# Two stacked transformer blocks on one core: work at eight seams between stages, and the order inside attention, rearranged

## The chip, the core and the metric

The kernel runs on one core of one Trainium2 chip. The core has five engines with queues of their own: TensorE (PE; its weight loads, PEld, overlap the matmuls), VectorE (DVE), ScalarE (ACT), GpSimd (POOL) and SyncE (SP), which here issues nearly all DMAs. Each engine takes its instructions in order and waits on counting semaphores. The metric is the device time of one execution in microseconds. All data are float32.

## The reference

The input is x (512 tokens of width 1024), a context of 256 tokens and conditioning vectors. Two blocks follow each other:

```
first_block:   h = modulate(rms_norm(x))
               hgrn2 branch: 4 heads, chunked gated linear scan, both directions
               deltanet branch: 4 heads, 2-D conv, gated delta rule, both directions
               x = x + g1 * (concat(gated_head_norm(o) for both branches) @ w_out)
               x = x + g2 * hierarchical_moe(modulate(rms_norm(x)))   # 16 experts, top 2
second_block:  layer 0: attention over ctx+lat (768 keys, 512 queries), then conv_ffn
               layer 1: sgu_mixer, then conv_ffn; last an rms_norm
gated_head_norm(o, gate, w) = rms_norm(o, w) * silu(gate)          # per head of 128
attention: 4 differential heads (two 64-wide maps each, p = p1 - lam * p2, then
           rms_norm over the head, *0.8) and 8 query heads of 64 on 2 KV heads;
           each layer: x = x + g1 * mixer(...);  x = x + g2 * conv_ffn(...)
sgu_mixer: z = gelu(h @ w_in); u, v = split(z); v = rms_norm(v)
           mixed = w_s (4 groups of 128x128, per chunk of 128 tokens) @ v + b_s
           return (u * mixed) @ w_out
conv_ffn:  z = h @ w_up; 3-tap conv over tokens; (silu(g) * u) @ w_down
```

## The kernel before, in words

**Stages.** The kernel is one program of thirteen stages in a fixed order: norm1, hg0, hg1, dn0, dn1, wout, moe, proj, attn, awout, ffn0, sgu, ffn1. Each engine has its own function for each stage (`pe_attn`, `act_attn`, `dve_attn`, `pool_attn`, and so on), and the order within an engine is written out by hand. After each stage every engine but SP calls `meet` (L207 to L211):

```
def meet(eng, who):
    k = meetings[who] = meetings.get(who, 0) + 1
    eng.drain().then_inc(s["stage_done"], 1)
    eng.wait_ge(s["stage_done"], 4 * k)
```

So none of the four starts a stage before all have ended the one before. SP isn't in the meetings; it runs ahead with the weight chunks (1 MB each, a ring of six slots, `Stream`), and waits for `stage_done` in two places, after moe (for attention's small tables) and after ffn0 (for sgu's).

**Tiles.** Tokens are in four tiles of 128 (NX = 4). `hT` holds the normed input transposed (8 chunks of 128 channels by 512 tokens), `xres` the residual, `ps` is PSUM with eight banks of 512 floats a partition. One product of a stage (`L694`, `L2450`, `L3029`) is eight contraction steps of 128 into one 128 x 256 block; a 128 x 512 one is in two halves of 4 steps. Each float32 matmul shows as two records in the trace.

**dn1.** The inverse of the delta rule's triangular systems is a loop of units u over levels and chunks (DVE L1588, POOL's masks L1416, PE L1173 to L1201), then come five state steps k (PE L1221 to L1247, POOL's `kx` L1458), then the outputs of four chunks (DVE L1648, semaphore `do_out`).

**The output stages** wout (j = 0), awout (j = 1) and the end of sgu (j = 2) share `pe_out`, `act_out`, `dve_out`, `pool_out`. `pe_gate_rows` (L476) makes the gate of all channels a row of every partition with 32 small matmuls into banks 0 to 3; ACT copies them out (`gate_rows_out`). For each token tile m: DVE prepares the source (`prep`), PE turns it (L1724), ACT and DVE copy the turned halves to `hT`, PE does two half products (L1734, 16 records each), DVE multiplies by the gate (L1802), POOL adds to `xres` (L1832), ACT sums the squares (L1681), DVE scales by the root (L1701), PE turns that tile again (L1674, the renorm) and ACT and DVE write it with scale and shift to `hT` (L1688, L1706), where the next stage reads it. The renorm of tile m - 1 stands behind the products of tile m, that of the last tile behind all.

**prep** of wout is: square, sum over each of eight heads, mean and epsilon, (ACT: root), times the silu gate `gz`, times the norm's weight in two halves, reciprocal, product (L1876 to L1885). That of awout does the same for the four differential heads (L2723 to L2731), that of sgu adds the bias to the mixed values and multiplies (L3085).

**proj and attention.** proj makes 36 products of 128 x 256 in six banks; the other two take heads being turned (L2466). Attention has 32 units: (group g, head h, query tile m); g = 0 are the differential heads, g = 1 the grouped ones. A unit is: scores of two maps over 768 keys into banks 0 to 3 (L2592, each map on its own 64 rows of the array), two maxima on DVE (L2663), two exps on ACT (L2643), reciprocals (L2684), for g = 0 the combination on DVE (L2687, L2689), for g = 1 a scaling of one map on DVE (L2694) and of the other on POOL (L2701), the turns of the probabilities (L2607), their copies (ACT L2652 and L2654, DVE L2681), the product with the values (L2619 or L2623) and its copy out (L2671, L2673). PE's order is scores u + 1, values u - 1, turns u.

**ffn.** Each pair of 128-wide column blocks of w_up is computed by seven products of half size (L2842) instead of eight, from sums and differences of weights (`weight_sums`, L2928 to L2932) and of token halves (`xsum`, L2935 to L2939). Products 0 and 1 take the first 256 tokens as they are; product 2 is the first that needs sums. Then come the down products, with the second half tile by tile and the renorms behind (layer 0).

**sgu.** 32 products of 128 x 256, each through Gelu (L3057), the four column groups of v first; then gate rows, the turn of the mixing weights (L3040), the four mixes (L3048, 8 records each) and `pe_out` with j = 2.

## Time and profile before

| what | value |
|---|---|
| median of 3 runs | 2980.68 us (2980.64 to 2988.81) |
| profiled execution | 2980.87 us, its span 2978.8 us |
| PE busy | 2763.9 us, 93% |
| DVE, ACT, POOL busy | 39%, 21%, 16% |
| mean granted clock of TensorE | 0.972 |
| DMA | 403.12 MB, mean 135 GB/s |

The span is from the first to the last instruction that the profiler recorded. A row of the timeline merges neighbouring instructions of one kind: start, time, engine, line, what it writes and reads, how many, and in brackets how long the engine had been idle and who released it. The granted clock is TensorE's in shares of full speed; it has two levels, 1.0 (2.4 GHz) and 0.5 (1.2 GHz), and values between are means over a stretch.

### The profile page before, as it was taken

Reading aid. Unit: us, or ns where it says so; the run is one execution under the profiler, and the core shown is the slowest. Engines: PE = TensorE matmul, PEld = TensorE weight load, DVE = VectorE, ACT = ScalarE, POOL = GpSimd, SP = SyncE. Lnnn points to the kernel's source line nnn. Section 1 sums busy time; section 2 is a strip of 40 time slices with the busy share of each in tenths; the row PEclk is TensorE's granted clock in tenths of the full one; section 3 lists DMA queues with packets and bytes.
Section 4 is the critical chain, followed back from the end, with each engine's and each line's share of the span. In section 5 each row is a group of like instructions: output and inputs, shape, how many; then the busy total and the mean of one; then the engine's idle time right before and its main releaser. Section 6 shows DMA issues by size and latency. Waiting matters only on the chain.

```text
span 2978.8 us, 35816 instructions
## 1 busy us (share of the span) xinstructions
PE 2763.9 (93%) x14509; PEld 2052.2 (69%) x14509; DVE 1168.4 (39%) x2158; ACT 613.9 (21%) x1186; POOL 465.5 (16%) x499
## 2 busy tenths in 40 slices
PE   7999988988985999999999887899999999999998
PEld 4676655776752788788778665588864685788843
DVE  2173662663353111111134575476720002677601
ACT  2102021332312111111131354121100121211100
POOL 2152502636401000000010023111101001011100
PEclk9999998999997999999999999999999999999999
DMA  9211141434632999999952100122221320322220
GB/s 371 88 43 43 67 171 46 142 128 144 213 117 101 354 331 334 320 330 335 319 176 71 43 1 1 57 90 94 85 66 48 111 84 15 120 85 85 78 78 28
DMA packets 202879, 403.12 MB, mean 135 GB/s; under 512 B 12882, under 2 KB 100482, under 8 KB 193538
## 3 DMA queue, kind: packets, MB, share of 16 engines
q1 hardware_dynamic: 195554, 375.15, 36.7%
q10 hardware_dynamic: 4896, 17.83, 1.5%
q0 software_dynamic: 2304, 8.39, 0.7%
q8 instruction: 89, 1.46, 0.2%
q14 instruction: 36, 0.29, 0.0%
HBM read 369.88 MB, written 31.46 MB: 135 GB/s over the span
## 4 chain that ended last, share of the span: by engine, by line
PE 69%; issue 21%; DVE 4%; ACT 3%; DMA 1%; POOL 1%; ACTq 0%; SPq 0%; POOLq 0%; DVEq 0%
PE ps L2842 18%; PE ps L702 7%; PE ps L1734 5%; PE ps L2856 5%; PE ps L2450 4%; PE ps L3029 4%; PE ps L2871 4%; PE ps L694 3%; PE ps L393 2%; PE ps L1173 2%; PE ps L1187 2%; PE ps L774 2%; PE ps L2592 2%; DMA ring<-in_w_mod 1%; ACT arena L2643 1%
## 5 line engine op out<-in xcount | busy, mean ns | idle before, releaser
L2021 PEld LDWEIGHTS ps<-arena,ring 128*128 128x128 f32 x2944 | 334.3, 193 | 13.5 <-issue 10.5
L2021 PE MATMUL ps<-arena,ring 128*128 128x128 f32 x2944 | 334.6, 276 | 2.6 <-DMA ring<-in_w_gate 2.6
L2842 PE MATMUL ps<-arena 128*128 128x256 f32 x1056 | 235.3, 379 | 3.2 <-DVE arena L2939 3.2
L2842 PEld LDWEIGHTS ps<-arena 128*128 128x128 f32 x1056 | 200.5, 190 | 31.2 <-DVE arena L2939 4.0
L1734 PE MATMUL ps<-ring,hT 128*128 128x512 f32 x384 | 173.7, 609 | 4.1 <-DVE arena L3085 2.6
L702 PE MATMUL ps<-hT,ring 128*128 128x512 f32 x384 | 172.1, 603 | 4.6 <-ACT ring L1312 2.1
L2842 PE MATMUL ps<-hT,ring 128*128 128x256 f32 x704 | 163.3, 386 | 3.3 <-ACTq L210 3.3
L2039 PE MATMUL ps<-ring,arena 128*128 128x512 f32 x368 | 164.0, 598 | 1.8
L2856 PE MATMUL ps<-ring,arena 128*128 128x512 f32 x352 | 151.5, 592 | 1.3 <-issue 1.3
L2842 PEld LDWEIGHTS ps<-hT,ring 128*128 128x128 f32 x704 | 136.4, 194 | 23.3 <-ACTq L210 4.1
L2871 PE MATMUL ps<-ring,arena 128*128 128x512 f32 x352 | 151.7, 592 | 0.0
L1416 POOL TENSOR_TENSOR arena<-arena,levm 128x256 f32<-128x256 f32 x168 | 128.8, 789 | 93.7 <-PE ps L1173 81.7
L1734 PEld LDWEIGHTS ps<-ring,hT 128*128 128x128 f32 x384 | 73.7, 196 | 91.7 <-issue 89.4
L2988 POOL TENSOR_TENSOR arena<-arena 128x512 f32<-128x512 f32 x44 | 56.7, 1288 | 509.8 <-DVE arena L2949 509.8
L2310 DVE TENSOR_TENSOR arena<-arena,ps 128x512 f32<-128x512 f32 x23 | 15.8, 687 | 303.9 <-PE ps L2021 303.9
L702 PEld LDWEIGHTS ps<-hT,ring 128*128 128x128 f32 x384 | 73.1, 193 | 89.8 <-issue 83.5
L2450 PE MATMUL ps<-ring,hT 128*128 128x256 f32 x576 | 125.3, 379 | 1.6 <-ACTq L210 1.6
L2039 PEld LDWEIGHTS ps<-ring,arena 128*128 128x128 f32 x368 | 68.0, 190 | 84.2 <-issue 84.2
L2856 PEld LDWEIGHTS ps<-ring,arena 128*128 128x128 f32 x352 | 66.7, 190 | 85.2 <-issue 85.2
L2871 PEld LDWEIGHTS ps<-ring,arena 128*128 128x128 f32 x352 | 66.7, 190 | 83.2 <-issue 83.2
L2450 PEld LDWEIGHTS ps<-ring,hT 128*128 128x128 f32 x576 | 109.0, 190 | 16.5 <-ACTq L210 1.9
L3029 PE MATMUL ps<-ring,hT 128*128 128x256 f32 x512 | 113.4, 385 | 1.6 <-ACTq L210 1.6
(485 smaller groups left out, 4196.6 us busy)
## 6 DMA issues: line engine op xcount, KB each, us to landing
ring<-in_ada_w SPq DMA_DIRECT2D x48, 1024.0 KB, 4.9
ring<-in_w_gate SPq DMA_DIRECT2D x46, 1024.0 KB, 7.2
ring<-in_w_up SPq DMA_DIRECT2D x46, 1024.0 KB, 6.5
ring<-in_w_down SPq DMA_DIRECT2D x46, 1024.0 KB, 5.3
ring<-in_ffn_w_up SPq DMA_DIRECT2D x44, 1024.0 KB, 5.1
ring<-in_w_mod SPq DMA_DIRECT2D x24, 1024.0 KB, 7.5
ring<-in_ffn_w_down SPq DMA_DIRECT2D x20, 1024.0 KB, 5.0
ring<-in_w_in SPq DMA_DIRECT2D x18, 1024.0 KB, 7.4
```

Of the source, the lines that this page charges most:

```text
L393: last = pe.matmul(ps[32 * b:32 * b + 32, mod_bank(g), :], sil[:, k, :], w[:, 0, b * BANK:(b + 1) * BANK], start=(k == 0), stop=(k == KD - ...
L694: last = pe.matmul(ps[:, bank, 0:CW], hsrc[:, k, m * P:(m + 1) * P], w[:, k, :], start=(k == 0), stop=(k == KD - 1))
L702: last = pe.matmul(ps[:, bank, 0:n], w[:, k, j * P:(j + 1) * P], src[:, k, :], start=(k == 0), stop=(k == KD - 1))
L1416: last = g.tensor_tensor(al[u % 2][:, 2 * d:2 * d + 2, :], AT[:, c, 2 * d:2 * d + 2, :], bc(levm[:, l, d, :], [P, 2, P], 1), ALU.mult)
L1734: last = pe.matmul(ps[:, 2 * (m % 2) + half, :], hT[:, 4 * q + k, m * P:(m + 1) * P], ws[2 * half + q][:, k, :], start=(q == 0 and k == 0) ...
L2021: last = pe.matmul(ps[:, t, f * P:(f + 1) * P], w[:, k, f * P:(f + 1) * P], xg[:, 4 * c + k, :], start=(c == 0 and k == 0 and f == 0), sto ...
L2039: last = pe.matmul(ps[:, 2 + half, :], aT[:, 2 * c + k, :], w[:, k, half * 512:(half + 1) * 512], start=(c == 0 and k == 0), stop=(c == 1 ...
L2450: last = pe.matmul(ps[:, u % PB, 0:CW], hT[:, k, m * P:(m + 1) * P], w[:, k, :], start=(k == 0), stop=(k == KD - 1))
L2842: last = pe.matmul(ps[:, u % 8, 0:HTOK], a[:, k, :], b[:, k, :], start=(k == 0), stop=(k == KD // 2 - 1))
L2856: last = pe.matmul(ps[:, m, :], fa[:, q + k, m * P:(m + 1) * P], w[:, k, :], start=(q + k == 0), stop=(q + k == NF - 1))
L2871: last = pe.matmul(ps[:, 4 + m, :], fa[:, q + k, m * P:(m + 1) * P], ws[i][:, k, :], start=(q + k == 0), stop=(q + k == NF - 1))
L3029: last = pe.matmul(ps[:, u % 8, 0:CW], hT[:, k, m * P:(m + 1) * P], w[:, k, :], start=(k == 0), stop=(k == KD - 1))
```

## The change

`meet` gets a parameter that leaves the waiting out; it is left out behind dn1, proj, attn, awout, ffn0 and sgu, and the dependences that it covered have semaphores of their own. Pieces of one stage move into the neighbour:

- dn1 and wout: DVE squares and sums the four hg heads at four units of dn1's inverse (u = 8, 14, 20, 26); POOL multiplies the gates `gz` by the norm's weights behind the state steps k = 1 to 4; `prep` is left with half the square and sum. ACT loads the table of the root early and does tile 0's root ahead of the gate rows.
- proj and attention: banks are given out anew in proj's last eight products (`proj_bank`), so that scores 0 stand before product 33 and scores 1 before product 35, and the first exps between proj's last copies.
- attention: the scores are signalled and awaited by map; from unit 17 on DVE's copy of the turned probabilities stands behind the next reciprocal and scaling.
- attention and awout: squares and weights of the differential heads go to POOL, sums to DVE, the root to ACT, all in units 17 to 31; `prep` is one product.
- awout and ffn0, sgu's output and ffn1: `pe_ffn_ahead` puts products 0 and 1 ahead of the last renorm, the first weight sums stand around the last tile's scaling, and the token differences are signalled in two parts.
- ffn0 and sgu: `pe_sgu_ahead` puts sgu's product 0 ahead of the last renorm, and products 1 to 3 wait for tiles, not for the stage.
- sgu and its output: gate rows before product 14, the weights' turn before 25, mixes 0 to 2 before 28, 29, 30, mix 3 behind the first turn.

The diff, cut to its core:

```diff
-        def meet(eng, who):
+        def meet(eng, who, wait=True):
             eng.drain().then_inc(s["stage_done"], 1)
-            eng.wait_ge(s["stage_done"], 4 * k)
+            if wait:
+                eng.wait_ge(s["stage_done"], 4 * k)
...  (pool_dn, dve_dn)
+                if p and k:
+                    for b in range(2):
+                        x = gz[:, k - 1, 512 * b:512 * b + 512].rearrange("p (h x) -> p h x", x=P)
+                        last = g.tensor_tensor(x, x, bc(hgw[:, b, :], [P, 4, P], 1), ALU.mult)
+                if p and u in WO_SUMS_AT:
+                    ch.link(v.tensor_tensor(wo_sq[:, 0:4], x, x, ALU.mult))
+                    ch.link(v.reduce_sum(hss[:, m, 0:4], wo_sq[:, 0:4], axis=X))
...  (pe_out)
             turn(0)
+            if between:
+                between()
+            if j < 2:
+                pe.wait_ge(s["gate_out"], j + 1)
...
+            if ahead:
+                ahead()
             renorm(NX - 1)
...  (dve_wout)
-                ch.link(v.tensor_tensor(wo_sq, o, o, ALU.mult))
-                ch.link(v.reduce_sum(hss[:, m, :], wo_sq, axis=X))
+                ch.link(v.tensor_tensor(wo_sq[:, 4:8], o[:, 4:8], o[:, 4:8], ALU.mult))
+                ch.link(v.reduce_sum(hss[:, m, 4:8], wo_sq[:, 4:8], axis=X))
...
-                for b in range(2):
-                    ob = o[:, 4 * b:4 * b + 4, :]
-                    ch.mark(v.tensor_tensor(ob, ob, bc(hgw[:, b, :], [P, 4, P], 1), ALU.mult))
...  (proj)
+        def proj_bank(u):
+            return u % PB if u < 28 else 4 + u % 2 if u < 32 else 6 + u % 2
+                    if u in (32, 33):
+                        pe.wait_ge(s["heads_act"], (n + 1) // 2)
+                        pe.wait_ge(s["heads_dve"], n // 2)
...
+                    if u == 33:
+                        pe.wait_ge(s["ap_out"], CTX_UNITS + 28)
+                        attn_scores(pe, 0)
+                    if u == 35:
+                        attn_scores(pe, 1)
...  (attention)
+        def attn_scores(pe, u):
+            for a, c0, c1 in ((0, 0, BANK), (1, 0, BANK), (0, BANK, TOK), (1, BANK, TOK)):
+                if u and c0 == 0:
+                    pe.wait_ge(s["exp_done"], 2 * u - 1 + a)
+                last = pe.matmul(...)
+                if c1 == TOK:
+                    last.then_inc(s["score2_ps"], 1)
-                if 1 <= u <= AU:
-                    (wait, copy of the turned probabilities of u - 1)
+                if 1 <= u <= ND or u == AU:
+                    turn_out(u - 1)
                 if u < AU:
                     (reciprocals, combination or scaling)
+                if ND < u < AU:
+                    turn_out(u - 1)
...  (pool_attn, i = u - 16)
+                if 1 <= i <= 2 * NX:
+                    m, weighed = divmod(i - 1, 2)
+                    if not weighed:
+                        g.tensor_tensor(ao_sq[m % 2], o, o, ALU.mult).then_inc(s["probs_pool"], 1)
+                    else:
+                        g.tensor_tensor(o, o, bc(subw[:, :], [P, 4, P], 1), ALU.mult).then_inc(s["probs_pool"], 1)
...  (ffn)
+        def pe_ffn_ahead(pe, W, l):
+            pe.wait_ge(s["h2_act"], renormed(2 + 2 * l, 2))
+            pe.wait_ge(s["h2_dve"], renormed(2 + 2 * l, 2))
+            pe.wait_ge(s["gated"], 8 * (1 + l) + 6)
+            for u in range(2):
+                up_product(pe, W, u, *seven_products(w, 0)[u])
...  (dve_ffn; the products wait for the first part at 2, for the second at 3)
+            ch.link(v.tensor_tensor(xsum[:, 0], tokens_part(0, 1), tokens_part(0, 0), ALU.subtract))
+            v.wait_ge(s["h2_act"], renormed(2 + 2 * l, NX))
+            v.tensor_tensor(xsum[:, 1], tokens_part(1, 1), xsum[:, 0], ALU.subtract).then_inc(s["sums_ready"], 1)
...  (pe_sgu)
+                if u == 14:
+                    pe.wait_ge(s["gelu_out"], 12)
+                    pe_gate_rows(pe, 2, False)
+                if u == 25:
+                    (turn of the mixing weights)
+                if 28 <= u < 31:
+                    mix(u - 28)
+                sgu_unit(pe, W, w, u)
+            pe_out(pe, W, 2, so, lambda: pe_ffn_ahead(pe, W, 1), lambda: mix(3))
```

## Rows read from the trace of the kernel before

**Rows 1.** The page: busy us (share) and instructions; the chain that ended last.
```profile
PE 2763.9 (93%) x14509; PEld 2052.2 (69%) x14509; DVE 1168.4 (39%) x2158; ACT 613.9 (21%) x1186; POOL 465.5 (16%) x499
...
PE 69%; issue 21%; DVE 4%; ACT 3%; DMA 1%; POOL 1%; ACTq 0%; SPq 0%; POOLq 0%; DVEq 0%
```
**Rows 2.** Windows: stretch, length, busy of PE, PEld, DVE, ACT, POOL, granted clock, DMA.
```profile
1691.00:1754.00 63.00, 51.03 (x358) 37.26 (x356) 53.33 (x95) 32.61 (x70) 0.00 (x0) 1.00 0.00 1
```
**Rows 3.** Waits (us in all, times, longest) and timeline of PE around wout.
```profile
PE ps L1724 <- DVE arena L1885: 6.4, 3, 5.3
...
843.47 3.84 PE L480 MATMUL ps<-ident,modv 128*128 128x128 f32 x32 [1.81 <-DVEq L210]
...
855.40 9.66 PE L1734 MATMUL ps<-ring,hT 128*128 128x512 f32 x16 [0.83 <-ACT hT L1765]
...
880.94 7.03 PE L1734 MATMUL ps<-ring,hT 128*128 128x512 f32 x16
```
**Rows 4.** Timeline of DVE and ACT, start of wout.
```profile
843.51 1.23 DVE L1876 TENSOR_TENSOR arena<-arena 128x1024 f32<-128x1024 f32 x1
...
847.36 1.29 DVE L1882 TENSOR_TENSOR arena<-arena,hgw 128x512 f32<-128x512 f32 x2
...
847.41 2.06 ACT L1864 ACTIVATE gate<-ps 128x512 f32<-128x512 f32 x4 [14.89 <-PE ps L480]
```
**Rows 5.** Timeline of PE and DVE, end of proj and attention's start.
```profile
1657.23 13.98 PE L2450 MATMUL ps<-ring,hT 128*128 128x256 f32 x64
...
1677.66 2.93 PE L2592 MATMUL ps<-arena 64*128 64x512 f32 x8 [4.39 <-ACT arena L2643]
...
1691.13 1.82 DVE L2663 TENSOR_REDUCE bet<-ps 128x1 f32<-128x768 f32 x2 [0.15 <-PE ps L2592]
```
**Rows 6.** Timeline of DVE and ACT, a unit of attention's first half.
```profile
1741.88 1.82 DVE L2663 TENSOR_REDUCE bet<-ps 128x1 f32<-128x768 f32 x2 [0.15 <-PE ps L2592]
...
1743.83 0.89 ACT L2643 ACTIVATE arena<-ps,bet 128x768 f32<-128x768 f32 x1
...
1746.47 1.82 DVE L2663 TENSOR_REDUCE bet<-ps 128x1 f32<-128x768 f32 x2 [0.15 <-PE ps L2592]
```
**Rows 7.** Timeline of POOL and DVE, attention's last half.
```profile
1764.74 2.60 POOL L2701 TENSOR_SCALAR arena<-arena,bet 128x768 f32<-128x768 f32 x1 [2.55 <-DVEq L2693]
...
1768.98 0.69 DVE L2681 COPY arena<-ps 128x512 f32<-128x512 f32 x1 [1.64 <-PE ps L2607]
```
**Rows 8.** Line L1832: ns min/median/max; and its longest in the timeline.
```profile
L1832 POOL TENSOR_TENSOR xres<-xres,arena x24: 1262/1270/2179, 866.0 to 2540.8; 128x512 f32<-128x512 f32 x24
...
873.61 2.18 POOL L1832 TENSOR_TENSOR xres<-xres,arena 128x512 f32<-128x512 f32 x1 [6.34 <-DVE arena L1802]
```
**Rows 9.** Timeline of PE, start of awout.
```profile
1848.67 1.09 PE L1724 MATMUL ps<-ident,arena 128*128 128x128 f32 x4 [5.69 <-DVE arena L2731]
1850.45 8.79 PE L1734 MATMUL ps<-ring,hT 128*128 128x512 f32 x16 [0.69 <-ACT hT L1765]
```
**Rows 10.** Timeline of PE and DVE, end of awout and start of ffn0.
```profile
1915.39 1.94 PE L1674 MATMUL ps<-ident,arena 128*128 128x128 f32 x8 [4.13 <-DVE arena L1701]
1918.96 5.25 PE L2842 MATMUL ps<-hT,ring 128*128 128x256 f32 x16 [1.63 <-ACTq L210]
1926.28 5.45 PE L2842 MATMUL ps<-arena 128*128 128x256 f32 x24 [2.07 <-DVE arena L2939]
...
1921.48 1.22 DVE L2935 TENSOR_TENSOR arena<-hT 128x1024 f32<-128x1024 f32 x1
```
**Rows 11.** Timeline of PE, end of ffn0 and start of sgu.
```profile
2347.50 1.06 PE L1674 MATMUL ps<-ident,arena 128*128 128x128 f32 x8 [3.94 <-DVE arena L1701]
2350.20 30.10 PE L3029 MATMUL ps<-ring,hT 128*128 128x256 f32 x126 [1.63 <-ACTq L210]
```
**Rows 12.** Timeline of PE, end of sgu's products and its output.
```profile
2468.41 7.17 PE L3048 MATMUL ps<-arena 128*128 128x256 f32 x32 [0.78 <-DVE arena L3080]
...
2479.01 8.53 PE L1734 MATMUL ps<-ring,hT 128*128 128x512 f32 x16 [2.56 <-DVE arena L3085]
```

More of the change, by code:

```diff
@@ L1803, in gated @@
                                 ALU.mult).then_inc(s["gated"], 1)
-            prep(0)
-            if early > 2:
-                prep(1)
+            before = 1 if early == 2 else NX - 1
+            for m in range(before):
+                prep(m)
             dve_turn_out(v, j, 0)
-            for m in range(1 if early == 2 else 2, early):
+            for m in range(before, early):
                 prep(m)
@@ L1820, in dve_out @@
                     prep(m + 2)
+                if spare and m == NX - 1:
+                    spare(0)
                 dve_xn(v, ch, m)
+            if spare:
+                spare(1)
             dve_renorm_out(v, NX - 1, which, out_bank(NX - 1))
@@ L1868, in root @@
                 a.activation(hss[:, m, :], hss[:, m, :], ACT.Sqrt).then_inc(s["stage_root"], 1)
+            root(0)
+            a.wait_ge(s["mod_done"], MGROUPS)
+            gate_rows_out(a, 0, lambda o, x: a.activation(o, x, ACT.Copy))
             act_out(a, 0, root)
@@ L2640, in act_attn @@
                         a.wait_ge(s["pt_ps"], u - 1)
[L2641 to L2645 removed]
+                    if u:
+                        attn_exp(a, u)
+                if u == AU:
+                    a.wait_ge(s["stage_mean"], SUB0)
+                    a.activation(ass, ass, ACT.Sqrt).then_inc(s["stage_root"], 1)
                 if u >= 1:
@@ L2918, in act_ffn, with weight_sums @@
             act_ffn_tail(a, l)
-        def dve_ffn(v, ch, l):
-            n0 = 4 * NPAIR * l
-            PAIRS = 2 * NPAIR
-            def weight_sums(n):
-                w, (slot, loads) = up_chunks[l][n]
-                S = [wsum[:, n % 2, i] for i in range(4)]
+        def weight_sums(v, ch, l, n, part=None):
+            w, (slot, loads) = up_chunks[l][n]
+            S = [wsum[:, n % 2, i] for i in range(4)]
+            if part != 1:
                 v.wait_ge(s[f"chunk_in{slot}"], loads)
```

350 lines of the change are left out of this document (206 added, 144 removed).

## The prediction

> **What bounds the kernel now.** I read the page first [rows 1]: TensorE is busy in 2763.9 us of the span of 2978.8 us, so what isn't its work is 215 us, and the chain that ended last runs over PE and its issue for 90%. No other engine is above 39%. So only TensorE's idle stretches, and its stretches at the low clock, can be worth anything. The reader is to see next, in the timeline of PE and in its waits, where a stage ends and the next begins: there the idle times are of 2 to 6 us, each with a name behind it (a norm's chain on DVE, the stage's meeting, a table load), and behind most of them the same matmuls take longer, since the granted clock stands at 0.5 (1.2 GHz) for some microseconds. The third place is attention, where the clock is full in the windows [rows 2] but PE waits once in each unit.
>
> The profiled execution took 2980.87 us (span 2978.8 us, 2.1 us around it); the median of the runs is 2980.68 us, so the sum is taken from 2980.9.
>
> **dn1 to wout.** Before: when the last delta-net output is written, DVE begins square (1.23), sum, scale, gate (1.22), weight (1.29 for two), reciprocal and product (1.23) for the first token tile; PE, which had the gate rows in front, waits for it, three times 6.4 us in all, 5.3 the longest; the first half product starts at 855.40 and its 16 matmuls take 9.66 us at the low clock, where 16 others take 7.03 [rows 3, 4]. After: the squares and sums of the four hg heads are taken inside dn1's inverse, the weights are multiplied by POOL there, a dummy Sqrt loads the table early. The chain left is half a square and half a sum (0.65 each), 0.17, the gating 1.22, 0.2 and 1.23: from 843.4 it ends at 847.6, just as the gate rows are done (843.47 + 3.84). The next to be late is ACT: its four gate copies (2.06) and then its copy of the turned tile (0.6) end near 850.2. So the product starts 5.2 us earlier; between are no idle times over 1.6 us, so I take the clock as full: 2.6 us more. The two later waits in the 6.4 (1.1 us) go, since a tile's preparation falls from 6.5 to 4.0 us beside half products of 7. What it adds: 8 DVE instructions of 0.65 us in the inverse, in which DVE idles 1.5 us or more between units, and 8 POOL products in the state steps, where POOL idles over 4 us a step; kx of the next step queues behind two of them (2.6 us) with a step of slack. I take 0.5 us lost (bounds 0 and, if each DVE pair delays a unit by its whole 1.25, 5). Term 8.4 us, bounds 3 and 9.5.
>
> **proj to attention.** Before: proj's last product ends at 1671.2, the first scores start at 1671.72, the second at 1677.66 after a table load and a whole softmax, all at the half clock; DVE's maxima of unit 3 start at 1691.13 [rows 5]. After: scores 0 stand before proj's 34th product, scores 1 before the 36th. PE then ends proj later: two score blocks (1.5 each), plus 1 us at product 33, which now waits until the turned heads are out of banks 6 and 7; a product is 3.45 (64 matmuls in 13.98 [rows 5]). That gives 1675.2. ACT copies that product first, so exp 1 runs 1675.7 to 1677.6, scores 2 follow, maxima 2 start at 1679.3, maxima 3 one unit later at 1683.8. Term 7.3 us; bounds 5 (the start is at half clock again) and 9.
>
> **Attention, first 16 units.** A unit takes 4.59 us (the maxima start at 1741.88 and 1746.47) [rows 6]. "Scores by maps" lets the first map's 512 columns start after the first exp, and the first maximum after the first map. But DVE's own loop is maximum 0.95, exp, exp (1.05 + 0.89 + 1.01 from its start), reciprocal, the two multiply-adds (0.2 + 0.25 + 1.02): 4.44. Only DVE's wait of 0.15 goes; 13 units give 2.0 us. Bounds 0 and 2.4.
>
> **Attention, last 16.** A unit takes 5.16 us (POOL idles 2.55 and works 2.60, again and again). The loop: POOL 2.60, turns 1.5, DVE's copy 0.69, reciprocal, POOL again [rows 7]. The change puts DVE's copy of the unit before behind the reciprocal and product of this one, so POOL no longer waits for the turns. Next comes PE: scores 1.49, values 1.45, turns 1.44, together 4.4, and DVE's loop with the copy 4.5: about 4.55. 15 units by 0.6 are 9.0. Against it: four sums of 0.72 on DVE and a few tiny ones, about 3.0 on its loop. POOL's own new products (1.27 by the nearest row [rows 8]) go with 2.60 into 4.55. Term 6.0 us; bounds 0 and 9.
>
> The row [rows 8] shows that such a POOL product can also take 2.18 us: that one, at 873.61, began inside a DVE product with two operands in SBUF (873.45 to 874.67). The Trainium skill says of this (SBUF — State Buffer, section "SBUF: two separate sides") that DVE and GpSimd hold a shared port pair for a whole instruction and the other one blocks; the trace agrees with these 0.9 us. It speaks against the change, which puts 16 POOL products beside DVE's work, and is rival A.
>
> **Attention to awout.** Before: PE's first turns wait 5.69 us for a chain with a table load in it; the first half product starts at 1850.45 and takes 8.79 [rows 9]. After: squares and weights are on POOL, sums and root in the last units, one product of 0.69 is left and done before PE's last values. PE: gate rows from 1838.8, 3.84, turns 1.0; ACT's gate copies and turn end near 1845.4, which starts the half product: 5.0 us, and 1.8 for the clock. Term 6.8, bounds 4.9 and 7.
>
> **awout to ffn0, and sgu to ffn1** (the same chain twice, 16.06 us from the third renorm to the third product in both). Before: PE waits 4.13 for the last tile's norm, turns it, meets, runs two products of 8 matmuls (5.25 at the half clock, 3.45 at full), waits 2.07 for the token differences, and goes on at 1926.28 [rows 10]. After: the two products need only the first 256 tokens and stand in the wait; the weight sums (2.7 on DVE) stand around the last tile's norm. DVE is then late: its half of the last tile ends at 1918.0, two differences of 1.22 end at 1920.5, the third product starts at 1920.6, and the fourth would wait 0.7 for two more differences. Without the clock that is 5.0 us; PE idles 4 us before it, as long as the idle time that brought the low clock in [rows 10], so I take 1.0 off. Term 4.0 twice; bounds 2.5 and 5.5 each.
>
> **ffn0 to sgu.** Before: 3.94 idle, turns, meeting, products from 2350.20, of which 126 take 30.10 where 27.2 would be full clock [rows 11]. After: product 0 stands in the wait (it needs DVE's part of tile 2, 2344.7), then the last turns, then the rest without a gap; product 1 starts at 2349.2 instead of an equivalent of 2356.5. Term 7.2; bounds 4.4 (clock as before) and 7.4.
>
> **Inside sgu.** Gate rows, weight turns and the four mixes (3.6 + 0.6 + 7.17) move behind products, at no cost of their own: the work is the same. Before, from 2463.45 to the end of the first half product are 23.9 us, with waits of 0.78 and 2.56 and the 8.53 in it [rows 12]. After: 3.6 + 0.6 + 5.4 of it between products, 0.7 for the last Gelu, turns 1.0, the fourth mix 1.75 (it hides the copies), 7.03: 20. Term 4.0; bounds 2.5 and 4.5. ACT's gate copies (2.06) and squares, moved forward, have eight banks' slack.
>
> Sum: 8.4 + 7.3 + 2.0 + 6.0 + 6.8 + 4.0 + 4.0 + 7.2 + 4.0 = 49.7 us; 2980.9 - 49.7 = 2931 us. All low ends together leave 25 us of gain (2956), all high ends 60 (2921). No DMA is on the path: SP's waits on the meetings of moe and ffn0 stay, and the chunks in question were loaded before the stage began (PE's waits there name no DMA).
>
> **Rivals.** A, the port: each of 8 units of attention's last half gets up to 0.9 us longer on POOL or DVE, 7 us: 2938. For it: the one row of 2.18; against it: no DVE operation of these units has two SBUF operands but for the small ones. Chance 0.10. B, the maps no longer overlap: the two maps' matmuls use different halves of the array's rows and take 1.49 together, where 4 of 0.43 and 4 of 0.215 in a row are 2.58. If the separate waits part them always, PE's unit in the last half is 5.5, above today's 5.16: the term turns from -6 to +8 and the 2.0 go: 2947. Against it: both exps are over when PE comes to them there. Chance 0.08. C, the clock is as low behind each seam as before (2.6 + 1.8 + 2.9 + 1.5, and the waits that it stretches): 2941. Chance 0.13. D, slower: the gaps, now more and shorter, hold the granted clock at half through attention. Units 1 to 3 had it so and took 5.9 instead of 4.59 (1.3 by 14), and PE's 4.4 of the last half would be 8.8 (4.3 by 15): 83 us, 3014. It decides from the point where over half of the units stand at 0.5; against it stands 1.00 in the windows with PE busy 0.81 of the time [rows 2]. Chance 0.02. E, the work is moved but another wait takes each place (an in-order engine with the new work in front): within 0.3%, which is about what a measurement of this kernel can tell from no change. Chance 0.02; a further 0.01 for slower by it.
>
> My forecast has 0.64. Range 2919 to 2953: it holds A, B and C. Faster by over 0.3%: 0.95; within: 0.02; slower: 0.03.
>
> **What would show it.** In the trace after: the first half product of wout some 5 us after the last delta-net output plus gate rows, in about 7 us; no idle time over 2 us between attention and proj; units of 4.45 and 4.55 us; in the tail of awout and of sgu's output two products right behind the third renorm, and an idle time of about 4 us after the fourth; sgu's products without low clock. It is wrong if attention's last half keeps 5.16, if the scores take 2.5, or if PE's idle time in all falls by less than 25 us.

## The result, and the profile after

The changed kernel takes 2935.75 us (median of 4 runs, 2933.55 to 2936.43), the kernel before 2980.66 in the same series. The ratio is 0.9843, with an interval of 0.9824 to 0.9861: 45 us less, where 49.7 were forecast. The profiled execution took 2933.55 us with a span of 2931.8 us.

First the page: busy time and instructions, and the chain that ended last.
```profile
PE 2760.7 (94%) x14509; PEld 2056.7 (70%) x14509; DVE 1157.0 (39%) x2138; ACT 613.1 (21%) x1184; POOL 484.0 (17%) x515
...
PE 72%; issue 20%; DVE 3%; ACT 2%; DMA 2%; POOL 1%; SPq 0%; ACTq 0%; POOLq 0%; DVEq 0%
```
Beside [rows 1] PE has the same 14509 matmuls and 3 us less of busy time, so 44 of the 47 us of span were idle time of PE. DVE has 20 instructions fewer, POOL 16 more: eight products with the weights in dn1, four squares and four products with the weights in attention. PE bounds it as before.

Next the waits of PE from attention to the end (us in all, times, longest):
```profile
PE ps L2902 <- DVE arena L3047: 8.3, 2, 4.2
PE ps L2687 <- issue: 4.0, 5, 0.8
PE ps L2687 <- ACT arena L2719: 2.9, 2, 1.7
PE ps L1749 <- ACT gate L2798: 2.3, 1, 2.3
PE ps L1689 <- DVE arena L1716: 1.5, 2, 0.8
PE ps L3144 <- DVE hT L1721: 1.3, 1, 1.3
```
The three waits of 3.9 to 4.1 us for the last tile's norm are gone or 0.8 us long, and the table load at attention's start is away from PE. What stays is one wait of 4.16 us at each feed-forward seam, 2.3 us at attention's output, and in attention's last half five waits of 0.8 us and, for its last two units, waits of 1.7 and 1.2 us for ACT's copies.

The timeline of PE at wout, which answers to [rows 3] (start, length, engine, line, operation, count, and in brackets the idle time before it):
```profile
849.25 1.09 PE L1739 MATMUL ps<-ident,arena 128*128 128x128 f32 x8 [0.42 <-DVE arena L1908]
851.59 7.11 PE L1749 MATMUL ps<-ring,hT 128*128 128x512 f32 x16 [1.24 <-ACT hT L1786]
```
The gate rows start at 845.00, DVE's chain lets PE go on 0.42 us behind them, and the half product runs at full clock (granted 1.00), 7.11 us instead of 9.66 (granted 0.73 on average).

Attention: the scores of a unit of the first half on PE; DVE's maxima of units 3, 15 and 16; and two units of the last half on POOL and DVE (answering to [rows 5 to 7]):
```profile
1677.69 2.22 PE L2645 MATMUL ps<-arena 64*128 64x512 f32 x8
...
1675.38 1.81 DVE L2736 TENSOR_REDUCE bet<-ps 128x1 f32<-128x768 f32 x2
...
1727.77 1.81 DVE L2736 TENSOR_REDUCE bet<-ps 128x1 f32<-128x768 f32 x2
1732.11 1.81 DVE L2736 TENSOR_REDUCE bet<-ps 128x1 f32<-128x768 f32 x2
...
1741.12 1.82 DVE L2736 TENSOR_REDUCE bet<-ps 128x1 f32<-128x768 f32 x2 [0.36 <-PE ps L2645]
1742.12 1.03 POOL L2792 TENSOR_TENSOR arena<-arena 128x512 f32<-128x512 f32 x1
...
1744.93 0.68 DVE L2767 TENSOR_REDUCE stat<-arena 128x4 f32<-128x512 f32 x1
1745.64 0.69 DVE L2729 COPY arena<-ps 128x512 f32<-128x512 f32 x1
1746.25 1.81 DVE L2736 TENSOR_REDUCE bet<-ps 128x1 f32<-128x768 f32 x2
1746.97 1.27 POOL L2794 TENSOR_TENSOR arena<-arena,hgw 128x512 f32<-128x512 f32 x1
```
A unit of the first half is 4.34 us (1732.11 - 1727.77), and DVE no longer waits for the scores. The scores of the two maps are spread over 2.22 us there, where they took 1.56 before the change; PE has no idle time left in these units (busy in all of the 56.73 us from unit 3 to unit 16). The loop over DVE and ACT closes in the same 4.34 us, so which of the two bounds the unit can't be told from this. In the last half the sum (0.68) stands in front of DVE's copy in four units; such a unit is 5.1 to 5.4 us long, the next one 4.4 to 4.7. POOL's square takes 1.03 us and its weight product 1.27.

PE at attention's output and at the start of ffn0 (answering to [rows 9, 10]):
```profile
1820.89 8.80 PE L1749 MATMUL ps<-ring,hT 128*128 128x512 f32 x16 [2.26 <-ACT gate L2798]
```
```profile
1880.66 1.04 PE L1689 MATMUL ps<-ident,arena 128*128 128x128 f32 x8
1881.53 3.62 PE L2902 MATMUL ps<-hT,ring 128*128 128x256 f32 x16
1885.90 1.06 PE L1689 MATMUL ps<-ident,arena 128*128 128x128 f32 x8 [0.75 <-DVE arena L1716]
1891.13 8.21 PE L2902 MATMUL ps<-arena 128*128 128x256 f32 x24 [4.16 <-DVE arena L3047]
1899.17 1.89 PE L2902 MATMUL ps<-arena,ring 128*128 128x256 f32 x8
...
2506.67 7.64 PE L2902 MATMUL ps<-arena 128*128 128x256 f32 x24 [4.16 <-DVE arena L3047]
```
The chain is shorter, but the first block behind each of these idle times runs in part at the low clock: 8.80 us where 7.0 is full (granted 0.80 on average, and 0.61 in its first 3.6 us), 8.21 where [rows 10] has 5.45 for the same 24 matmuls (granted 0.65), and 7.64 for them at ffn1 (0.70). Where this text says that a block is at the low clock, it means such a part of it.

At sgu's start and in its output PE runs through (answering to [rows 11, 12]):
```profile
2312.45 3.69 PE L3144 MATMUL ps<-ring,hT 128*128 128x256 f32 x16 [1.27 <-DVE hT L1721]
2315.98 1.04 PE L1689 MATMUL ps<-ident,arena 128*128 128x128 f32 x8
2317.28 22.90 PE L3144 MATMUL ps<-ring,hT 128*128 128x256 f32 x105 [0.26 <-issue]
```
```profile
2434.23 1.09 PE L1739 MATMUL ps<-ident,arena 128*128 128x128 f32 x8 [0.47 <-ACT arena L3197]
2436.89 7.03 PE L1749 MATMUL ps<-ring,hT 128*128 128x512 f32 x16
```

### The profile page after: what moved, and what is told of

It reads as the page before. It is cut to its first block, busy times and chain, and to the rows that moved or that the text cites. A ratio compares the mean times of both kernels' runs of the same rounds, so it can differ in the third digit from the quotient of the medians.

```text
span 2931.8 us, 35814 instructions
## 1 busy us (share of the span) xinstructions
PE 2760.7 (94%) x14509; PEld 2056.7 (70%) x14509; DVE 1157.0 (39%) x2138; ACT 613.1 (21%) x1184; POOL 484.0 (17%) x515
## 4 chain that ended last, share of the span: by engine, by line
PE 72%; issue 20%; DVE 3%; ACT 2%; DMA 2%; POOL 1%; SPq 0%; ACTq 0%; POOLq 0%; DVEq 0%
PE ps L2902 18%; PE ps L703 8%; PE ps L1749 6%; PE ps L2954 5%; PE ps L2969 5%; PE ps L2488 4%; PE ps L3144 4%; PE ps L695 3%; PE ps L2645 2%; PE ps L1177 2%; PE ps L1191 2%; PE ps L394 2%; PE ps L775 2%; DMA ring<-in_w_mod 1%; PE ps L2669 1%
## 5 line engine op out<-in xcount | busy, mean ns | idle before, releaser
L2969 PE MATMUL ps<-ring,arena 128*128 128x512 f32 x352 | 151.7, 592 | 0.0
```

The source lines that it names most:

```text
L2969: last = pe.matmul(ps[:, 4 + m, :], fa[:, q + k, m * P:(m + 1) * P], ws[i][:, k, :], start=(q + k == 0), stop=(q + k == NF - 1))
```

## The ledger: each term against the two traces

Each row is how much earlier a landmark comes after the change than before it, less what the landmark ahead of it had already gained. Landmarks are starts of the same work in both timelines: "second turns" are those of the second token tile in an output stage, "product 1" and "product 5" are counted from 0 in sgu and in a feed-forward. The third renorm, used below, is the turns of the third token tile, the last ones that need not wait at a seam.

| term | forecast | measured | from |
|---|---|---|---|
| up to dn1's last output | 0 | -1.6 | 841.28 to 842.85 |
| dn1 to wout | 8.4 | 10.4 | moe's start 927.63 to 918.84 |
| moe | 0 | -0.3 | proj's first product 1536.65 to 1528.16 |
| proj to attention | 7.3 | 7.3 | maxima of unit 3, 1691.13 to 1675.38 |
| attention, first 16 units | 2.0 | 3.2 | maxima of unit 16, 1751.05 to 1732.11 |
| attention, last 16 | 6.0 | 5.5 | last values, 1837.18 to 1812.71 |
| attention to its output | 6.8 | 5.1 | second turns, 1859.08 to 1829.52 |
| output to ffn0 | 4.0 | 2.8 | product 5, 1931.57 to 1899.17 |
| ffn0 to sgu | 7.2 | 6.7 | product 1, 2356.35 to 2317.28 |
| inside sgu | 4.0 | 4.5 | second turns, 2487.37 to 2443.76 |
| sgu to ffn1 | 4.0 | 3.4 | product 5, 2561.16 to 2514.15 |
| sum | 49.7 | 47.0 | the spans, 2978.8 to 2931.8 |

Of the first row, -2.0 us already stand where dn1's inverse begins, ahead of which the change leaves the code alone (DVE's first subtraction there starts at 707.84 before and at 709.84 after).

## Experiments

All edit the kernel after, and ran four or five times each beside the kernel before. Executions of one kernel lie up to 13 us apart (last section), and the intervals of all kernels with a part undone overlap that of the kernel after. So the effect is read in one profiled execution of each, from proj's first product (1528.16) to the end (2931.8): 1403.6 us in the kernel after. In that stretch too the clock behind an idle time can differ from one execution to the next by up to 1.7 us at a place; where it does, the text says so.

| kernel | median us | ratio to before, interval | proj's first product to end | against after |
|---|---|---|---|---|
| after, again | 2939.7 | 0.9856, 0.9835 to 0.9877 | 1403.65 | 0.0 |
| meets_back | 2937.4 | 0.9850, 0.9836 to 0.9863 | 1406.1 | +2.4 |
| turn_copy_old | 2939.8 | 0.9856, 0.9841 to 0.9871 | 1407.2 | +3.6 |
| scores_whole | 2938.9 | 0.9857, 0.9838 to 0.9877 | 1407.1 | +3.4 |
| wout_prep_old | 2939.4 | 0.9853, 0.9838 to 0.9868 | 1403.4 | -0.2 (its edit lies ahead) |
| proj_scores_back | 2947.6 | 0.9861, 0.9839 to 0.9884 | 1407.4 | +3.7 |
| sgu_product_back | 2937.5 | 0.9846, 0.9829 to 0.9863 | 1407.1 | +3.5 |
| ffn_products_back | 2938.3 | 0.9842, 0.9823 to 0.9861 | 1401.3 | -2.4 |
| fill_idle | 2936.3 | 0.9846, 0.9829 to 0.9864 | 1399.9 | -3.8 |
| last_product_first | 2925.1 | 0.9807, 0.9792 to 0.9822 | 1393.6 | -10.1 |
| gates_before_values | 2929.4 | 0.9814, 0.9797 to 0.9830 | 1397.2 | -6.4 |
| three_together | 2919.6 | 0.9792, 0.9771 to 0.9812 | 1386.9 | -16.7 |

The kernel after, unchanged, ran again beside proj_scores_back, sgu_product_back and ffn_products_back, to show how far its own times go:

> The changed kernel, unchanged, beside the three others on the same chip: 2933 to 2937 us by every theory; it says how far its own times spread, and where in the kernel (by the times of proj's first product and of the end).

It took 2935.2 to 2943.2 us, more than expected, while from proj on it repeats to 0.01 us.

**Parts undone.** The meetings, `meet(pe, "pe", False)` and its like back to `meet(pe, "pe")` at four stages:

> Four of the six meetings that no longer wait (behind attention, the attention's output, ffn0 and sgu) wait again; the two behind dn1 and proj stay without a wait, and all moved work stays where it is. Theory: the gain came from the moved work, a waiting meeting only holds DVE and PE for the slowest engine's last instruction: about 1 us at attention's output, 0.5 to 1 us at each other seam, 3 us in all, so about 2939 us; the new PE waits are under 1.5 us each. Rival: the meetings themselves were the cost, and the moved work counts only since nobody meets: then 10 us or more come back, 2946 us or later.

Measured 2.4 us. Of these 0.4 lie at attention's output, 1.4 in sgu, where an idle time of 1.63 us stands in place of 0.26 (a little more than the 1.5 expected), and 0.1 at each feed-forward seam. The other 0.5 are the clock of the 24 matmuls behind the idle times (7.91 and 8.46 us against 8.21 and 7.64). These four meetings are cheap: nearly all of the gain at their seams is in the moved work. The two behind dn1 and proj were not put back.

**The copy of turned probabilities:**
```
-                if 1 <= u <= ND or u == AU:
+                if 1 <= u <= AU:
                     turn_out(u - 1)
...
-                if ND < u < AU:
-                    turn_out(u - 1)
```


> In attention's last 16 units DVE's copy of the turned probabilities of the unit before stands again in front of the reciprocal and the product of this one. Theory: POOL then waits for the turns again, and a unit takes 5.16 us as before the change, against 4.42 to 4.7 now: 0.6 us by 15 units, and the sums now lie in POOL's wait: 6 to 10 us more, about 2943 us, with POOL's idle time before its product back at about 2.5 us. Rival: the order of these two doesn't matter, the first map's earlier scores made the gain: within 1.5 us of 2936.

The timeline of POOL in the last half of this kernel:
```profile
1763.77 2.60 POOL L2784 TENSOR_SCALAR arena<-arena,bet 128x768 f32<-128x768 f32 x1 [1.31 <-DVEq L2761]
1766.34 1.04 POOL L2790 TENSOR_TENSOR arena<-arena 128x512 f32<-128x512 f32 x1
1768.93 2.60 POOL L2784 TENSOR_SCALAR arena<-arena,bet 128x768 f32<-128x768 f32 x1 [1.55 <-DVEq L2761]
```
A unit is 5.16 us again (1768.93 - 1763.77; 1774.08 and 1779.24 go on), with a sum in it or without: the sum then lies in POOL's loop. From proj's first product to the last values are 290.0 us instead of 284.55, so 5.5 us is what this one order brings, all of the term for the last half; 6 to 10 were expected. The rest of the kernel gave 1.9 back, 1.7 of them at attention's output, which with the same idle time in front ran at full clock here (granted 1.00).
```profile
1828.90 7.11 PE L1749 MATMUL ps<-ring,hT 128*128 128x512 f32 x16 [2.25 <-ACT gate L2796]
```

**The maps' scores awaited together:** `pe.wait_ge(s["exp_done"], 2 * u)` ahead of the first, one signal behind the last matmul.

> In attention a unit's scores wait for both exps of the unit before, and DVE's first maximum waits for both maps' scores, as before the change; the order of the four matmuls, the copy behind the reciprocal and all else stay. Theory: a unit of the first 16 takes 4.59 us again instead of 4.34 (0.25 by 13 or 14, 3.4 us), the last 16 lose at most 1 us, since both exps are over when PE comes to the scores: 2938 to 2940 us. Rival: the maps only overlapped less, and the first 16 units owe their 4.34 us to something else, such as scores issued in another order: unit 4.34 stays, within 1 us of 2936.

```profile
1677.05 1.82 DVE L2735 TENSOR_REDUCE bet<-ps 128x1 f32<-128x768 f32 x2 [0.15 <-PE ps L2645]
```
DVE's old wait of 0.15 us is back and the unit is 4.58 us. Up to the last values it costs 4.06 us: 0.5 ahead of unit 3, 3.2 in the first half, 0.4 in the last. The theory holds. To the end it is 3.4, since the 24 matmuls at the two feed-forward seams took 7.84 and 7.46 us here.

**The preparation of wout back in wout** (all eight heads squared and summed, and weighted, by DVE):
```
-                ch.link(v.tensor_tensor(wo_sq[:, 4:8], o[:, 4:8], o[:, 4:8], ALU.mult))
+                ch.link(v.tensor_tensor(wo_sq, o, o, ALU.mult))
...
+                for b in range(2):
+                    ob = o[:, 4 * b:4 * b + 4, :]
+                    ch.mark(v.tensor_tensor(ob, ob, bc(hgw[:, b, :], [P, 4, P], 1), ALU.mult))
```


> In wout the squares and sums of all eight heads and the products with the weight are DVE's again, in wout itself; dn1 has none of them. The table load for Sqrt stays early, the meeting stays away. Theory: the first token tile's chain grows by 0.6 + 0.6 + 1.3 us = 2.5 us, which the gate rows don't hide any more, and the preparation of tiles 2 and 3 (6.5 us) just fits beside two half products: 2.5 us, and up to 2.5 more if the clock falls to half before the first half product; 2938.5 to 2941 us. Nothing comes back in dn1: its additions cost nothing. Rival: the additions to dn1 delay its chain, so dn1's last output is written 2 us or more earlier without them, and the sum is zero.

```profile
858.15 1.77 PE L1728 MATMUL ps<-ident,arena 128*128 128x128 f32 x8 [2.81 <-DVE arena L1898]
...
860.90 9.25 PE L1738 MATMUL ps<-ring,hT 128*128 128x512 f32 x16 [0.98 <-DVE hT L1783]
```
The idle time ahead of the first turns is 2.81 us instead of 0.42, and the turns and the half product are slow: from the start of the gate rows to the last renorm are 77.65 us, against 72.84 in the second execution of the kernel after, whose half product was at the low clock too (in the first, with a full clock, 71.14): 4.8 us, the upper end of what was expected. To moe's start it is 3.9 us (80.34 against 76.41), since the last tile's turns behind their idle time of 4.13 us took 1.06 us here and 1.94 there.

The rival was that the additions delay dn1. It is settled between two landmarks: from DVE's first subtraction of dn1's inverse to dn1's last output are 133.45 us without the additions, and with them 133.01 and 133.44 in the two executions of the kernel after (133.44 in the kernel before). The additions cost nothing that shows.

**The scores of units 0 and 1 back behind proj:**

> The scores of units 0 and 1 and the first two exps stand again behind proj's last product, in attention's own stage; no meeting waits, proj's banks stay as changed. Theory: the idle times at attention's start return: two softmaxes in a row with a table load, so the maxima of unit 3 start 21 to 22 us behind proj's 33rd product instead of 15: 5 to 7 us more against the last product, about 2942 us. Rival: the missing meeting was the gain, and the first exps are hidden from PE by nothing else either: under 2 us more, 2938 us or less.

The maxima of unit 3 come 151.7 us behind proj's first product instead of 147.2: 4.5 us, somewhat less than expected, with the idle time back on PE (2.06 us) and one of 16 us on DVE. To the end it is 3.7, since the 24 matmuls at the two feed-forward seams took 7.79 and 7.43 us here. The rest of the term of 7.3, 2.8 us, isn't tested; the missing meeting and the banks given out anew are the parts of the change that are left there.

**sgu's first product back behind the last turns:**

> In ffn0's tail sgu's first product (1.75 us at full clock) stands behind the last tile's turns instead of before them; no meeting waits. Theory: PE waits 4 us for the last tile's norm again (now 0.8), and since product 0 then fills the wait for the copies behind the turns (1.27 now), the loss is 3.2 + 0.2 - 1.3 us, some 2 us, and 2 to 3 more if the idle time of 4 us brings the low clock, as it did before: 2938 to 2941 us. Rival: the moved product was all of the 6.7 us of this seam: 6 us or more, 2942 us.

```profile
2314.21 1.06 PE L1689 MATMUL ps<-ident,arena 128*128 128x128 f32 x8 [3.93 <-DVE arena L1716]
2315.11 5.30 PE L3144 MATMUL ps<-ring,hT 128*128 128x256 f32 x16
2320.67 19.66 PE L3144 MATMUL ps<-ring,hT 128*128 128x256 f32 x90 [0.26 <-issue]
```
Product 1 starts 11.4 us behind the third renorm (2309.24) instead of 7.1: 4.3 us, 1.6 of them in the low clock of product 0 (5.30 instead of 3.69). My expectation mistook the product's length, which is 3.45 us and not 1.75. The rival, 6 us or more, is out: the other 2.4 us of this seam's 6.7 were left in place, and which part of the change brings them isn't tested.

**The feed-forward's two products back behind the last turns:**
```
-            if ahead:
-                ahead()
             renorm(NX - 1)
+            if ahead:
+                ahead()
```


> At both feed-forward seams the two products that stand before the last tile's turns stand behind them again; the weight sums stay early and no meeting waits. Theory: the third product waits for DVE's two differences either way, so the idle time of 4.16 us only moves from behind the turns to before them: it starts at the same 10.5 us behind the third renorm. Without an idle time right before it its 24 matmuls take 5.4 to 6.5 us instead of 8.21, while the first two are slower (5.2 instead of 3.6) and may be done later: from -2.5 to +1.5 us for each seam, and I expect -1 at each, about 2934 us. Then this part of the change, by itself, gained nothing, and the 2.8 and 3.4 us of the term were the early weight sums and the missing meeting. Rival: the moved products are the gain: 2.5 us or more lost at each seam, 2941 us.

```profile
1896.34 1.32 PE L1689 MATMUL ps<-ident,arena 128*128 128x128 f32 x8 [4.20 <-DVE arena L1716]
1897.45 5.09 PE L2902 MATMUL ps<-hT,ring 128*128 128x256 f32 x16
1902.91 5.42 PE L2902 MATMUL ps<-arena 128*128 128x256 f32 x24 [0.37 <-issue]
1908.17 1.89 PE L2902 MATMUL ps<-arena,ring 128*128 128x256 f32 x8
```
Product 5 starts 17.06 us behind the third renorm (1891.11) instead of 18.51, and at ffn1 17.06 instead of 17.95: this part of the change loses 1.45 and 0.89 us at the two seams. They differ as the 24 matmuls of the kernel after do there (8.21 and 7.64 us). The idle time was not filled but moved to where more work stands behind it: ahead of the turns it slows 8 turns and 2 products (0.3 + 1.5 us), ahead of the third product it slows three (2.8 us).

**Is the low clock due to the idle time?** PE repeats the first product twice in the 4.16 us:
```
+            for r in range(2):
+                for k in range(KD // 2):
+                    a, b = seven_products(chunks[0][0], 0)[0]
+                    pe.matmul(ps[:, 2 + r, 0:HTOK], a[:, k, :], b[:, k, :], start=(k == 0), stop=(k == KD // 2 - 1))
```


> In each of the two idle times of 4.16 us ahead of the feed-forward's third product (in ffn0 and ffn1) PE repeats the feed-forward's first product twice, into a bank that is overwritten later; its result isn't used. All else is as after the change. Theory: the low clock of the 24 matmuls behind it (8.21 and 7.64 us where full clock is 5.4) comes from this idle time, so they take 5.4 to 5.6 us: 2.2 to 2.8 us each, 4 to 5 in all, about 2931 us. Rival: the clock is low for what came before the idle time, or the matmuls would be slow for another reason: 8.2 us stays, within 1 us of 2936.

```profile
1892.16 1.97 PE L2902 MATMUL ps<-arena 128*128 128x256 f32 x8 [0.34 <-DVE arena L3051]
1894.47 3.72 PE L2902 MATMUL ps<-arena 128*128 128x256 f32 x16 [0.34 <-DVE arena L3054]
1898.02 1.89 PE L2902 MATMUL ps<-arena,ring 128*128 128x256 f32 x8
```
The three products take 5.69 us of work instead of 8.21 (granted 1.00), and product 5 comes 16.33 us behind the third renorm (1881.69) at both seams, instead of 18.51 and 17.95. So the idle time made the clock. What is now seen is that DVE's differences are next (0.34 twice).

**Work that needs no difference first.** The order of the first seven products:
```
+        FIRST_ORDER = (0, 1, 6, 4, 2, 3, 5)
...
-                for p, (a, b) in enumerate(seven_products(w, n)):
+                seven = seven_products(w, n)
+                for p in (range(7) if n else FIRST_ORDER):
+                    a, b = seven[p]
```


> In both feed-forwards the seven products of the first pair of chunks run in the order 0, 1, 6, 4, 2, 3, 5: product 6 needs no token difference, only the last renormed tile and a weight sum that is ready, product 4 only the first difference. The consumers wait for the same products. Theory: PE goes on 1.5 us after the last tile's turns instead of 4.16, product 6 starts 7.9 us after the third renorm, the differences (1.23 each) are then ahead of PE, and with an idle time of 1.5 us the clock stays full: the seven products end 16.5 to 17 us after the third renorm instead of 22.0, 5 us at each of the two seams, 10 us in all, about 2926 us. Rival: the low clock comes whatever the idle time, then the products still take 2.6 us each for three of them: 2.6 us at each seam, about 2931 us. Second rival: DVE is late again for product 2 or 3, an idle time of 1 us or more inside.

```profile
1882.23 1.04 PE L1689 MATMUL ps<-ident,arena 128*128 128x128 f32 x8
...
1890.20 1.97 PE L2904 MATMUL ps<-hT,arena 128*128 128x256 f32 x8 [1.67 <-ACT hT L1703]
1892.01 5.34 PE L2904 MATMUL ps<-arena 128*128 128x256 f32 x24
```
The idle time is 1.67 us, the clock stays full, and the seven products end 16.68 us behind the third renorm (the next chunk's first product starts at 1898.91) instead of 21.97: 5.3 us. At ffn1 it is 16.69 instead of 21.41, 4.7 us, together 10.0. The median is 10.6 us below that of the kernel after (2925.1, with five runs within 1.7 us), and the intervals, 0.9792 to 0.9822 and 0.9824 to 0.9861, don't touch.

**Gate rows ahead of the last values** (`pe_gate_rows(pe, 1, False)` between the last turns and `values(AU - 1)`):

> The gate rows of attention's output stand before the last unit's values instead of behind them. Theory: they fill PE's wait of 1.18 us for the copies of the last turned probabilities, ACT's gate copies (2.06) lie beside the values, and the first half product starts 2.3 to 2.8 us earlier against the last turns, with an idle time of under 1 us in front of it instead of 2.26: 2.5 us if the clock was full there anyway, 4.3 if it was low (8.80 us instead of 7.1 for the half product): 2931.5 to 2933.5 us. Rival: the values and DVE's copy of the last unit then come later and hold the first half product, which needs them: nothing gained, within 0.7 us of 2936.

```profile
1823.72 7.10 PE L1749 MATMUL ps<-ring,hT 128*128 128x512 f32 x16 [0.73 <-ACT hT L1786]
```
The idle time in front is 0.73 us instead of 2.26, and the half product is at full clock: from proj's first product to ffn0's third renorm 348.0 us instead of 352.5, 4.5 us. The other 1.9 us of the 6.4 are not its own: this execution's 24 matmuls behind the idle times of 4.16 us took 6.96 and 7.01 us instead of 8.21 and 7.64.

**All of it together**, with only tile 0 squared, summed and weighted inside attention's units:

> last_product_first and gates_before_values together, and in attention's last half only the first token tile is squared, summed and weighted inside the units; the other three tiles' squares, sums and weights are DVE's in the stage of the output, where DVE idles 14 us. Theory: the units that hold a sum (5.4 us against 4.4 to 4.7) fall to the others' length, three of them, 2 to 3 us; DVE's preparation of tile 1 ends over 2 us before its turns. With 10 and 2.5 to 4.3 us of the other two: 2919 to 2922 us. Rival: the sums weren't what lengthened those units (POOL's squares and weights, or PE's own order, were): then the units stay and it ends at 2922 to 2924; and if the pieces share one gain (a clock that falls somewhere else instead), 2926 or later.

The starts of PE's values in three units of the last half:
```profile
1763.59 1.53 PE L2695 MATMUL ps<-arena 128*64 128x128 f32 x24
...
1768.00 1.53 PE L2695 MATMUL ps<-arena 128*64 128x128 f32 x24
...
1772.69 1.53 PE L2695 MATMUL ps<-arena 128*64 128x128 f32 x24
```
The one unit that still holds a sum is 5.42 us long and the next 5.31; from there on the units are 4.41 and 4.69 us in turn. ffn0's third renorm comes 345.8 us behind proj's first product: 2.2 us less than with the gate rows alone, what three sums were worth. The product order ends the seven products 16.7 us behind the third renorm at both seams again. In all 16.7 us from proj on, against 4.5 + 2.2 + 10.0 = 16.7 added up. The median of 2919.6 us (2914.5 to 2927.6) beats the kernel after by 16 to 20 us; the ratio intervals, 0.9771 to 0.9812 and 0.9824 to 0.9861, don't touch.

## Why the prediction was right, and where its terms were off

The mechanism was right: PE's idle time fell by 44 us at nearly the same busy time, and all nine terms have their sign and place, and most their size. The total is 2.7 us less than forecast. 1.9 of that is no term at all (the stretches up to dn1's last output and moe); the nine terms together are 48.9, with errors from -1.7 to +2.0, so part of the closeness is that these cancel, which is luck.

**dn1 to wout, 8.4.** The chain was as worked out (DVE done just behind the gate rows, product 1.24 us behind ACT's copy). The term assumed the full clock. The profiled execution had it, and gave 10.4; 0.9 of that is the last tile's turns, 1.07 us instead of 1.94 behind the same idle time of 4.13 us, which the term didn't name. But of the twelve profiled executions with this code ten had the low clock in the half product; the second one of the kernel after shows it:
```profile
850.26 8.80 PE L1749 MATMUL ps<-ring,hT 128*128 128x512 f32 x16 [1.25 <-ACT hT L1786]
```
There, from the gate rows to moe's start are 76.4 us instead of 73.8, and the term is 7.8. The price of 0 to 5 us for dn1's additions is nothing, and the 0.5 taken off for it were too much; undoing the preparation alone costs 3.9 to 4.8.

**proj to attention, 7.3.** Right, and 4.5 of it is shown to be the moved scores and exps.

**Attention's first half, 2.0.** The step that DVE's loop is 4.44 us long was wrong: it added up durations, but a maximum starts 0.04 to 0.09 us before the operation ahead of it ends. The starts themselves give 4.34. So not only the wait of 0.15 went, but 0.25 a unit, 3.2 in all, and undoing the maps' separation gives exactly that back.

**Attention's last half, 6.0.** 5.5, all of it from the order of DVE's copy. The length of 4.55 worked out from the bound (PE 4.4, DVE 4.5) is the mean of three_together's 4.41 and 4.69; a sum makes a unit and the next together 9.8 us instead of 9.1, so four cost 2.9, where 3.0 were taken off for them.

**Attention to its output, 6.8.** The step that failed is "and 1.8 for the clock". The wait for ACT's gate copies was foreseen, but it leaves PE idle 2.26 us, and the half product is 8.80 us long, as before the change (8.79 in [rows 9]). Of the eleven profiled executions with this order ten have it at 8.75 to 8.80; the other is turn_copy_old with 7.11. gates_before_values shows both parts: less idle time, and 7.10.

**The two seams ahead of a feed-forward, 4.0 each.** 2.8 and 3.4. The idle time of 4.16 us was foreseen, its price not: 1.0 us was taken off, and the 24 matmuls behind it lost 2.8 and 2.2 (8.21 and 7.64 against 5.4). fill_idle shows that it is the idle time. A deeper error is in the reason for the gain: "the two products stand in the wait". They do, and that loses 1.45 and 0.89 us by itself; without it both seams gain 4.3 us. The rows of DVE say where that comes from, though no run undoes it singly. Its first token difference starts 7.8 us behind the third renorm instead of 11.3 (with the two products in either place), since the weight sums are done before it and no meeting stands there; and the third product waits for two of the four differences instead of all, which is 2.2 us more.

**ffn0 to sgu, 7.2, and inside sgu, 4.0.** 6.7 and 4.5. In the first, 4.3 us are shown to come from the moved product; product 1 starts 7.1 us behind the third renorm, where the prediction has 6.7. In the second the prediction's own addends make 20.1 and a gain of 3.8; the two traces give 4.5 between the landmarks.

**The rivals.** A, the port: in attention POOL's squares took 1.03 us and its weight products 1.27, never more. The Trainium skill says (SBUF — State Buffer, section "SBUF: two separate sides") that one of DVE and GpSimd blocks while the other holds the shared pair, if DVE's operation has two operands in SBUF or is in one of its two-port modes; beside these squares and products DVE reads PSUM, and the rows agree with that limit. POOL's scaling kept its 2.60, but all 16 begin together with DVE's own scaling (0.62), so its length alone isn't known. B, the maps: the scores of the first half did spread, from 1.56 to 2.22 us, but the unit got shorter all the same (4.34), and in the last half they took 1.56 to 1.71 and units without a sum fell to 4.4. C, the clock as low as before: of its four terms the 1.8 at attention's output came true, the 2.9 and the 1.5 in sgu did not, and the 2.6 at wout did not in the profiled execution but 1.7 of it did in ten of twelve. D, the low clock in attention: not seen, the granted clock is 1.00 from 1663 to 1812 us. E, another wait in each place: only at the two feed-forward seams and attention's output, as told above.

## What to carry to other kernels

An idle time that is moved is not removed: ask what runs behind it, since here the work that followed paid for the clock, and filling a hole with work from just behind it lost 2.3 us at two seams. The better question is which of the late work needs least of what is late: reordering seven products by their operands gave 10.0 us, where moving two of them was thought to give 8.0. And a loop's length is read from start to start, not by adding durations.

## What the runs showed of the hardware

The same code with the same idle time in front can run at full clock or in part at the low one. Attention's output behind 2.25 us idle took 8.80 us in the kernel after and 7.11 in turn_copy_old (granted 0.80 and 1.00); wout's half product behind 1.24 us 7.11 twice and 8.80 ten times. The 24 matmuls behind 4.16 us idle took between 6.96 us (granted 0.77) and 8.27, never the 5.4 of full clock, in the 16 seams profiled with exactly this wait; behind 1.65 to 1.67 us the eight matmuls of product 6 and these 24 were at full speed all four times (1.97 and 5.34), and behind 2.07 and 1.15 us in the kernel before the 24 were too (5.45). The Trainium skill says that the window in which the clock's monitor judges the activity is free-running (TensorE: Matmul & The Clock Gate, section "Part 1: The HAM clock gate"); that would let the phase decide, and no run here tests it.

wout's gate rows start anywhere from 843.05 to 852.66 us, though ahead of dn1 the code is the same in all. The mean granted clock of the first 100 us goes with it only roughly: 0.91 to 0.93 in the three executions that come to the gate rows behind 851 us, 0.95 to 0.98 in the others (843.05 to 847.39), without order among these. Two rows (the clock is the third number from the end):
```profile
0.00:100.00 100.00, 79.76 (x347) 52.92 (x348) 15.87 (x36) 23.21 (x43) 17.21 (x66) 0.98 0.91 331
```
```profile
0.00:100.00 100.00, 76.97 (x337) 53.63 (x338) 15.88 (x36) 23.05 (x43) 17.24 (x66) 0.91 0.92 331
```
The first is the second execution of the kernel after (gate rows at 843.67), the second proj_scores_back (852.66). That is the likely reason why the median of proj_scores_back stands 12 us above that of the kernel after while its effect is 4.5; only one of its five runs was profiled, but the mean granted clock of a whole run goes the same way (0.971 in the three of 2947.6 to 2948.0 us, 0.977 in that of 2934.7). What sets that clock at the start is open.
